# Expert-choice routers of a two-layer encoder: the chosen tokens numbered by sums with a triangular mask in place of an index search

## The reference

```python
def expert_choice_moe(h, w_router, w_gate, w_up, w_down):
    B, S, D = h.shape                       # 1, 256, 1024 per sequence
    T = B * S
    cap = EC_CAPACITY_FACTOR * T // N_EXPERTS   # 2 * 256 // 16 = 32
    xt = h.reshape(T, D)
    aff = jax.nn.softmax((xt @ w_router).astype(jnp.float32), axis=-1)
    gate, idx = lax.top_k(aff.T, cap)       # each of 16 experts takes its 32 best tokens
    xe = jnp.take(xt, idx, axis=0)
    hid = jax.nn.silu(jnp.einsum('ecd,edf->ecf', xe, w_gate)) * jnp.einsum('ecd,edf->ecf', xe, w_up)
    ye = jnp.einsum('ecf,efd->ecd', hid, w_down) * gate[..., None].astype(h.dtype)
    out = jnp.zeros_like(xt).at[idx.reshape(-1)].add(ye.reshape(-1, D))
    return out.reshape(B, S, D)
```

## Time and profile before

| | |
|---|---|
| median of 3 runs | 1790.93 us (1790.51 to 1790.94) |
| profiled execution | 1791.96 us, of which the span of the trace 1790.2 us |
| mean granted TensorE clock | 0.978 |
| TensorE matmul busy | 1644.9 us, 92% of the span |
| VectorE busy | 515.9 us, 29% |
| ScalarE busy | 461.8 us, 26% |
| DMA | 450.30 MB, mean 252 GB/s |

### The profile page before, as it was taken

How to read it: one execution, slowest core, us unless ns; L and a number is a source line. 1 busy time by engine, 2 the same in 40 slices (tenths; PEclk the granted TensorE clock), 3 DMA queues, 4 the chain that set the end, 5 groups by cost and what they waited for, 6 DMA issues and landing times.

```text
span 1790.2 us, 20467 instructions
## 1 busy us (share of the span) xinstructions
PE 1644.9 (92%) x8671; PEld 781.4 (44%) x8671; DVE 515.9 (29%) x998; ACT 461.8 (26%) x1008; POOL 67.5 (4%) x87
## 2 busy tenths in 40 slices
PE   7999799998899979999999999997999988999887
PEld 4464344342233324444445678853443422433233
DVE  3562411120201203255451355633111201112032
ACT  3232211110011005432234565442111010111053
POOL 2000000000000000000004232000000000000000
PEclk9999899999999999999999999999899999999999
DMA  7007279999999994012120000264599999999931
GB/s 248 1 9 320 118 292 427 428 427 428 428 424 427 428 421 155 1 47 94 47 94 1 2 2 2 96 268 179 215 430 427 426 429 428 423 427 428 427 141 47
DMA packets 50907, 450.30 MB, mean 252 GB/s; under 512 B 4932, under 2 KB 7200, under 8 KB 25600
## 3 DMA queue, kind: packets, MB, share of 16 engines
q1 hardware_dynamic: 50288, 448.67, 60.5%
q0 software_dynamic: 288, 0.22, 0.0%
q10 hardware_dynamic: 239, 0.09, 0.0%
HBM read 446.87 MB, written 2.10 MB: 251 GB/s over the span
## 4 chain that ended last, share of the span: by engine, by line
PE 72%; DMA 16%; ACT 4%; DVE 3%; issue 3%; POOL 1%; SPq 1%; DVEq 0%; ACTq 0%; POOLq 0%
PE banks L1727 26%; PE banks L1185 23%; DMA ring<-in_moe_w_up 7%; DMA ring<-in_moe_w_down 5%; PE banks L1378 4%; DMA ring<-in_moe_w_gate 3%; PE banks L1636 3%; PE banks L1706 3%; PE banks L1753 3%; PE banks L1781 2%; PE banks L1347 2%; PE banks L1268 1%; PE banks L1406 1%; PE banks L1428 1%; ACT xn L737 1%
## 5 line engine op out<-in xcount | busy, mean ns | idle before, releaser
L1727 PE MATMUL banks<-ring,misc 128*64 128x512 f32 x2048 | 458.6, 599 | 39.9 <-DMA ring<-in_moe_w_up 23.0
L1727 PEld LDWEIGHTS banks<-ring,misc 128*64 128x64 f32 x2048 | 146.6, 137 | 324.8 <-issue 279.3
L1727 PE MATMUL banks<-ring,hid_t 128*64 128x512 f32 x976 | 218.0, 596 | 18.3 <-DMA ring<-in_moe_w_down 15.6
L1185 PE MATMUL banks<-ring,xt 128*128 128x512 f32 (+1 forms) x448 | 189.8, 585 | 1.1 <-ACT xt L763 0.6
L2358 DVE TENSOR_TENSOR work<-work,banks 128x512 f32<-128x512 f32 x32 | 33.6, 1051 | 483.4 <-PE banks L1727 483.4
L1185 PE MATMUL banks<-xt,ring 128*128 128x512 f32 x384 | 166.7, 594 | 0.0
L1135 ACT ACTIVATE misc<-banks 32x512 f32<-32x512 f32 x64 | 37.5, 586 | 463.7 <-PE banks L1727 463.3
L1727 PEld LDWEIGHTS banks<-ring,hid_t 128*64 128x64 f32 x976 | 68.5, 137 | 158.6 <-issue 137.1
L1185 PEld LDWEIGHTS banks<-ring,xt 128*128 128x128 f32 x448 | 84.8, 190 | 104.0 <-issue 103.0
L1185 PEld LDWEIGHTS banks<-xt,ring 128*128 128x128 f32 x384 | 72.3, 190 | 91.8 <-issue 89.3
L2373 DVE COPY misc<-banks 32x512 f32<-32x512 f32 x64 | 44.2, 691 | 229.1 <-PE banks L1727 228.7
(11 more groups left out here) (311 smaller groups left out, 1533.8 us busy)
## 6 DMA issues: line engine op xcount, KB each, us to landing
ring<-in_moe_w_gate SPq DMA_DIRECT2D x64, 2048.0 KB, 22.3
ring<-in_moe_w_up SPq DMA_DIRECT2D x64, 2048.0 KB, 23.9
ring<-in_moe_w_down SPq DMA_DIRECT2D x58, 2048.0 KB, 25.1
ring<-in_gdn_w_in SPq DMA_DIRECT2D x8, 2048.0 KB, 8.6
ring<-in_ple_w_gate SPq DMA_DIRECT2D x4, 2048.0 KB, 21.5
ring<-in_moe_w_down SPq DMA_DIRECT2D x6, 1024.0 KB, 23.4
ring<-in_mla_w_out SPq DMA_DIRECT2D x2, 2048.0 KB, 23.7
misc<-in_moe_w_down SPq DMA_DIRECT2D x2, 2048.0 KB, 21.5
```

The source lines that it names most:

```text
L1185: mm = pe.matmul(psum[:, banks.bank(st, i), 0:cols], lhs(k), rhs(k), start=(k == 0), stop=(k == n - 1))
L1727: mm = pe.matmul(psum[64 * f:64 * f + 64, bank, :], tokens(4 * kh + k), w[k][:, k, f * HALF:(f + 1) * HALF], start=(kh == 0 and k == 0), s ...
```

## The change

The positions are no longer searched. On VectorE each of the four rounds is a maximum and an overwriting, the first of them straight from PSUM, and the last round overwrites too: what is then -1 is chosen. TensorE turns this back, so that tokens are on the partitions (stage `picked_t`), VectorE makes 1.0 or 0.0 of it (`picked`), and a product with a triangle of ones (`TRI_LE`), for the second half of a sequence also with all ones, counts for each token how many chosen tokens stand up to it. Multiplied with `picked` this is the token's place among the expert's 32 (`rank`), or zero. A comparison with 1 to 32 (`ramp`) gives the one-hots; it is now four instructions by groups of experts, each for all four matrices, and `gather(0)` waits for the first alone. The tokens of an expert are listed by position instead of by affinity.

While VectorE takes the maxima, TensorE runs four products of constants (`ident` with `tri`) whose result nobody reads.

The weights `gcol` come from 16 products of the one-hots with `aff` (`weigh`), four columns each. These, the turning of the one-hots and their scaling move from behind the down product of expert 0 to behind that of expert 2 (`ex == 3`). `aff`, `picked` and `rank` lie in `fac`, which is free then; `topi`, `topf`, `token` and `spread` are gone.

```diff
@@ TensorE
                 mm.then_inc(L.s_at.filled, 1)
+                banks.claim(pe, L.s_pk, 0)
+                for _ in range(4):
+                    pe.matmul(psum[:, banks.bank(L.s_pk, 0), :], ident[:, :], tri[:, :, :], start=True, stop=True)
                 pe.wait_ge(top_done, l + 1)
-                banks.claim(pe, L.s_gt, 0)
-                pe.transpose(psum[0:32, banks.bank(L.s_gt, 0), 0:32], topv[:, :], ident[0:32, 0:32]).then_inc(L.s_gt.filled, 1)
-                pe.wait_ge(spread_done, l + 1)
-                for s in range(NS):
-                    product(L.s_ib, s, lambda k: ones[0:32, :], lambda k: spread[:, 16 * s:16 * s + 16, :], 1, HALF)
-                pe.wait_ge(onehot_done, 4 * (l + 1))
+                for t in range(NT):
+                    mm = pe.transpose(psum[:, banks.bank(L.s_pk, 0), 32 * t:32 * t + 32], afft[:, t * P:(t + 1) * P], ident[0:32, 0:32])
+                mm.then_inc(L.s_pk.filled, 1)
+                L.s_pk.wait_read(pe, 0)
+                for t in range(NT):
+                    product(L.s_ib, t, lambda k: ones[:, :] if k < t else tri[:, TRI_LE, :], lambda k: picked[:, k, :], t + 1, 32)
                 L.s_ib.wait_read(pe, 1)
+                pe.wait_ge(onehot_done, 4 * l + 1)
...
+                def weigh():
+                    pe.wait_ge(moe_sem["gather_read_act"], 4 + L.done["gather_read_act"])
+                    for q in range(NQ):
+                        for s in range(NS):
+                            c0 = NS * GRP * q + GRP * s
+                            for t in range(NT):
+                                mm = pe.matmul(psum[:, 6, c0:c0 + GRP], oh[:, NT * s + t, q * P:(q + 1) * P], aff[:, t, s, GRP * q:GRP * q + GRP],
+                                               start=(t == 0), stop=(t == NT - 1))
+                    mm.then_inc(gcol_in, 1)
...
                         if i == 2 and q + 1 < NQ:
+                            pe.wait_ge(onehot_done, 4 * (l + 1))
                             gather(q + 1)
...
-                        if ex == 1:
-                            pe.wait_ge(gcol_done, l + 1)
+                        if ex == 3:
+                            pe.wait_ge(onehot_done, 4 * (l + 1))
+                            weigh()
                             for q in range(NQ):
                                 turn_onehot(q)
@@ VectorE
-                dve.tensor_copy(afft, psum[0:32, banks.bank(L.s_at, 0), 0:SEQ]).then_inc(L.s_at.freed(0)[0], 1)
-                L.s_at.wait_read(dve, 0)
+                left = psum[0:32, banks.bank(L.s_at, 0), 0:SEQ]
                 for r in range(CAP // 8):
-                    v8, i8 = topv[:, 8 * r:8 * r + 8], topi[:, 8 * r:8 * r + 8]
-                    link(dve.max(v8, afft))
-                    link(dve.max_index(i8, v8, afft))
+                    v8 = topv[:, 8 * r:8 * r + 8]
+                    link(dve.max(v8, left))
+                    ins = dve.match_replace(afft, v8, left, -1.0)
+                    left = afft
                     if r < CAP // 8 - 1:
-                        link(dve.match_replace(afft, v8, afft, -1.0))
...
+                ins.then_inc(top_done, 1)
+                dve.wait_ge(*L.s_pk.full(1))
+                dve.tensor_scalar(picked, psum[:, banks.bank(L.s_pk, 0), 0:64].rearrange("p (n x) -> p n x", n=NT), 0.0, None,
+                                  ALU.is_lt).then_inc(L.s_pk.freed(0)[0], 1)
...
+                for q in range(NQ):
+                    dve.tensor_tensor(oh[:, :, q * P:(q + 1) * P].rearrange("p j (e c) -> p j e c", c=CAP),
+                                      rank[:, :, GRP * q:GRP * q + GRP].unsqueeze(3).to_broadcast([P, NJ, GRP, CAP]),
+                                      ramp[:, :].unsqueeze(1).unsqueeze(1).to_broadcast([P, NJ, GRP, CAP]),
+                                      ALU.is_equal).then_inc(onehot_done, 1)
                 def scatter_weights():
+                    dve.wait_ge(gcol_in, l + 1)
+                    g0 = psum[:, 6, 0:NQ * NS * GRP].rearrange("p (q s e) -> p q s e", q=NQ, s=NS)
+                    for i in range(GRP):
+                        ins = dve.tensor_copy(gcol[32 * i:32 * i + 32, :, :], g0[32 * i:32 * i + 32, :, :, i])
+                    ins.then_inc(gcol_done, 1)
...
-                        if ex == 1:
+                        if ex == 3:
                             scatter_weights()
```

More of the change, by code:

```diff
@@ L146, in trunk_kernel @@
         diag32 = sb("diag32", [P, 32])
-        token = sb("token", [P, NT])
         gains = sb("gains", [P, 64])
@@ L202, in trunk_kernel @@
         sg, hid = work[:, 0:HALF], work[:, HALF:D]
-        aff = work[:, 0:64].rearrange("p (n s e) -> p n s e", n=NT, s=NS)
+        aff = fac[:, 0, :, :].rearrange("p j e -> p (j e)").rearrange("p (n s e) -> p n s e", n=NT, s=NS)
+        picked = fac[:, 1, :, :].rearrange("p j e -> p (j e)").rearrange("p (n x) -> p n x", n=NT)
+        rank = fac[:, 2, :, :]
         afft = work[0:32, 64:320]
@@ L207, in trunk_kernel @@
         topv = sb("topv", [32, CAP])
-        topi = sb("topi", [32, CAP], U32)
-        topf = sb("topf", [32, CAP])
+        ramp = sb("ramp", [P, CAP])
         gcol = sb("gcol", [P, NQ, NS])
-        spread = hid_t[0:32, :, :, :].rearrange("p a b w -> p (a b w)").rearrange("p (a c) -> p a c", c=CAP)
         first_down = misc[:, 2048:6144].rearrange("p (k w) -> p k w", k=4)
@@ L439, in trunk_kernel @@
             L.s_at = stage("aff_t", 1, ["dve"], before=L.s_lgt)
-            L.s_gt = stage("top_t", 1, ["dve"], before=L.s_at)
-            L.s_ib = stage("idx_rows", 2, ["dve"], before=L.s_gt)
+            L.s_pk = stage("picked_t", 1, ["dve"], before=L.s_at)
+            L.s_ib = stage("ranks", 2, ["dve"], before=L.s_pk)
             L.s_st = stage("scatter_t", 4, AV, before=prev and prev.s_st)
@@ L629, in _ @@
                 link(pool.memset(pick[:, b, b:b + 1], 1.0))
-            link(pool.iota(token[:, :], pattern=[[P, NT]], base=0, channel_multiplier=1,
+            link(pool.iota(ramp[:, :], pattern=[[1, CAP]], base=1, channel_multiplier=0,
                            allow_small_or_imprecise_dtypes=True))
@@ L1696, in gather @@
                             else:
-                                L.s_st.wait_read(pe, 2 + kp)
+                                who = ("act", "dve")[kp]
+                                pe.wait_ge(moe_sem["gather_read_" + who], 2 + L.done["gather_read_" + who])
                         if kp >= 2:
@@ L1739, in scatter @@
                 def scatter(q):
+                    if q == 0:
+                        L.s_st.wait_read(pe, 3)
                     pe.wait_ge(moe_sem["y_read_act"], GRP * (q + 1) + L.done["y_read_act"])
@@ L2324, in scatter_weights @@
-                def scatter_weights():
+                        link(ins)
+                    if r == 0:
+                        dve.sem_inc(L.s_at.freed(0)[0], 1)
+                ins.then_inc(top_done, 1)
+                dve.wait_ge(*L.s_pk.full(1))
+                dve.tensor_scalar(picked, psum[:, banks.bank(L.s_pk, 0), 0:64].rearrange("p (n x) -> p n x", n=NT), 0.0, None,
+                                  ALU.is_lt).then_inc(L.s_pk.freed(0)[0], 1)
+                L.s_pk.wait_read(dve, 0)
@@ new lines, in _ @@
+                for t in range(NT):
+                    dve.wait_ge(*L.s_ib.full(t + 1))
+                    dve.tensor_tensor(rank.rearrange("p (s n) e -> p s n e", s=NS)[:, :, t, :],
+                                      picked[:, t, :].rearrange("p (s e) -> p s e", s=NS),
+                                      psum[:, banks.bank(L.s_ib, t), 0:32].rearrange("p (s e) -> p s e", s=NS),
+                                      ALU.mult).then_inc(L.s_ib.freed(t)[0], 1)
+                L.s_ib.wait_read(dve, 1)
```

10 lines of the change are left out of this document (6 added, 4 removed).

## The result

The changed kernel takes 1775.73 us in the median of four runs (1775.0 to 1777.93), the kernel before beside it 1790.83. The ratio is 0.9919, with a 95% interval of 0.9904 to 0.9934: 15.1 us faster, where 14.0 were forecast (1776.9). The profiled execution took 1776.44 us with a span of 1774.7, against 1791.96 and 1790.2.

A forecast was written before the change was run, and what follows sets the result against it. The weight stream was taken to set the expert stage's end, starting only after router and gather. Savings there less the wait gave 6.9 + 7.1 = 14.0 us, so 1776.9 us; own range 1775.3 to 1778.5, wider range 1773.3 to 1781.2.

The forecast's parts named there:

- Selection: VectorE's choice of tokens in the router: four maxima and four overwritings take 3.84 us instead of 6.04, saving 2.20.
- From the turn back to the gather: Router, after the selection: turns, comparison, small products, multiplications and first quarter of one-hots take 2.65 us instead of 6.70, saving 4.05.
- The gather: TensorE's first gather, at full clock, takes 7.34 us instead of 9.40 and 9.59, saving 2.06 in layer 0, 2.25 in layer 1.
- The wait for the unread products: On TensorE after the selection: the four constant products run slow at first and delay the turn back by 1.4 us a layer.
- The halt at expert 3: TensorE's weight products, wait for copies and turning of one-hots: 7.8 us, 4.6 of them new, covered by DMA's backlog, cost 0.
- Sums: Total saved per layer, up to the first gate product: 6.9 us in layer 0, 7.1 in layer 1, together 14.0.
- the sign put down for this: In the experts, TensorE's first wait for a transfer should come near 400 minus 7, plus the delay of the added work.
- starting after one quarter: The gather starts after the first quarter of the one-hots; the other three, 2.1 to 3.2 us on VectorE, lie beside it.
- expert 1's missing stall: Moving the turning of the one-hots away from expert 1 removes a stall of 3.2 us there, which helps at 295.
- the thin one at 295: Place in the experts with the least DMA backlog: 26.2 MB issued against 24.4 moved, 4 us.
- the clock never falls: Rival: the unread products begin early enough to keep TensorE's clock and cost nothing; 16.8 us saved, 1774.1; chance 0.15.
- down again for the gather: Rival: TensorE's clock falls again before the gather; 12.5 us saved, 1778.4, or 9.7, 1781.2, with the wait; chance 0.17.

The follow-up runs named there:

- the second experiment: The changed kernel with the first gather waiting for all four comparisons, not the first alone: 1783.31 us, ratio 0.9956 to the kernel before.
- The longer halt: The changed kernel with 8 or 24 more unread products at the head of the halt behind expert 2's down product: 1780.73 and 1805.83 us.
- two later executions: The changed kernel with one unread product added just ahead of the gather, 1776.57 us; and with one during the softmax and five during the selection, 1776.63 us.
- every execution with an early product: Four variants of the changed kernel with one or two unread products added during the softmax, some with further ones later: 1779.41, 1779.02, 1776.43 and 1776.63 us.
- one early product: The changed kernel with one more unread product, during the softmax ahead of the turn of the affinities: 1779.41 us, ratio 0.9927 to the kernel before.

## Why the prediction was right

The bound, the places and the order of the sizes were as put. Step by step, with what was put first:

- *Selection:* 3.84, measured 3.93. The first round takes 1.08 from PSUM (208.06 to 209.14) and the later ones 0.96. Reading PSUM is not what costs: in layer 1 the first maximum and overwriting take 0.42 and 0.40 like those that follow. The 0.1 lies in the gap behind them, 0.14 in place of 0.03, where VectorE frees the bank; it is inside the bound of 0.3.
- *From the turn back to the gather:* 2.65, measured 2.58 in both layers. The first quarter of the one-hots took 0.691 and 0.693 us, the plain row's 0.693; the others begin 0.60 us apart. That I took the plain row and not the strided one was right. (The 0.625 in the expectation of the second experiment is not the duration of one.)
- *The gather:* 7.34, measured 7.38.
- *The wait for the unread products:* 1.4, measured 0.64 and 1.10. This term was too large. The clock came back 2.4 us after the products began in layer 0 and about 3.3 after in layer 1, where I had used 3.0 to 4.2, the 3.0 without a row for it.
- *The turn of the affinities:* not in the sum. In layer 0 it took 0.61 and not 0.41, as the clock had fallen before it.
- *The halt at expert 3:* 7.8 at no cost, measured 8.6 at no cost. The longer halt showed why. The backlog there was 21.5 us by the changed kernel's rows (43.0 MB issued up to 309, less 412 GB/s x 82 us = 33.8), where I had put 19 with the next piece.
- *Sums:* 6.9 and 7.1, measured 7.41 and 7.35. Layer 0: 2.11 for the selection + 4.12 for the way to the gather + 2.03 for the gather up to the first gate product - 0.64 for the wait - 0.21 for the slower turn. Layer 1: 2.11 + 4.12 + 2.22 - 1.10.

The mechanism was right, then, and the wait was the term that was off most. That the total came within 1.1 us owes something to luck: the changed kernel's own runs go from 1775.0 to 1777.93.

What the prediction missed did not show in the time. It said that TensorE meets the transfers at 399.87. But that row of the chain begins where the piece is issued, and TensorE waits only for its landing. Its own list (start us, us, what, idle us before) has the first waits of over 1 us for a transfer at 419.33 before and at 435.65 after:

```profile
419.33 3.65 PE L1727 MATMUL banks<-ring,hid_t 128*64 128x512 f32 x16 [1.15 <-DMA ring<-in_moe_w_down]
...
435.65 3.65 PE L1744 MATMUL banks<-ring,hid_t 128*64 128x512 f32 x16 [1.34 <-DMA ring<-in_moe_w_down]
```

So the sign put down for this (400 minus 7, plus the delay of the added work) did not come true: the first wait moved later. That the stream sets the end of the stage holds even so, by the 424.23 and 424.38 us of the two streams.

It also treated starting after one quarter as 2.1 to 3.2 us laid beside the gather, while the experiment prices it at 3.5 a layer, because the wait would also have cost the clock. And it put the move to expert 3 down as harmless, with expert 1's missing stall as a small help. The experiment shows that the new work at the old place would cost 4.6 and 4.5 us a layer, three fifths of the gain. Against the kernel before the move gains nothing by itself, as the streams are equally long; it is what keeps the gain. The backlog had been worked out for the new place and for the thin one at 295, but never for the new halt standing at the old place. There the prediction had the numbers (4 us of backlog against 4.6 more of halt) and did not use them.

Of the rivals, "the clock never falls" happened in one layer each of two later executions, and "down again for the gather" in at least one layer of every execution with an early product. The rule cited from the Trainium skill ("TensorE: Matmul & The Clock Gate", Part 4, that work in transpose mode does not count as busy) did not decide in the changed kernel, whose gathers ran at the full clock behind two turns and three small products. No run here shows the turns apart from the small products, so the rule itself is neither borne out nor refuted.

## What to carry to other kernels

When a stream of transfers sets the end of a stage, time ahead of its first freed place counts in full, and work behind it was free here only up to the backlog of issued transfers. That backlog is read from the profile as bytes issued less bytes moved, and it has to be worked out at the very place where the work is to stand, the following halt included. A row of the chain of waits that names a transfer begins at its issue, so look at the waiting engine's own list for when it waits. Products that nobody reads can pay, but where the clock falls differed here between layers with the same instructions: time such variants several times, and compare the stretches.

## What the runs showed of the hardware beyond what was expected

- In the variant that waits for all four comparisons TensorE stood for 2.9 us with nothing to do, at 2.4 GHz before, and the clock went down to 1.2 GHz as the gather began (0.80 in the 2 us around its start, then 0.50). In the changed kernel it did two turns and three small products ahead of the gather, and the gather ran at 1.00.
- In the halt at expert 3 TensorE had 32 products of four columns and sixteen turns to do. The clock was at 1.00 up to 311, at 0.95 up to 313, and at 0.50 from there to 319: it fell behind the products, about when TensorE waited 0.78 us for VectorE's copies, and stayed low through the turns.
- Some 3 us between profiles lie in layer 1's mixer, which no edit touched. From layer 0's first gate product to layer 1's turn of the affinities it is 1013.90 us in the changed kernel's first profile, 1014.24 in its second and 1017.17 with one early product. The last shows the clock at 0.91 and 0.92 from 735 to 755, where the others show 1.00; this dip holds 2 us of the difference, and the rest lies between 1015 and 1070.
